# Six rows of a vector-matrix product, moved part by part between the products that make the filters' taps

## The chip, the cores and the metric

The kernel runs on one core of one Trainium2 chip. The metric is the device time of one execution in microseconds, taken as the median of several runs. Inside a core five engines run their own instruction queues in order and wait for each other by semaphores: PE (TensorE, matrix products), DVE (VectorE), ACT (ScalarE), POOL (GpSimd) and SP (SyncE, which here only issues DMAs).

## What is computed

Two transformer-like blocks are applied to one sequence of 1024 positions and 1024 channels. The part that matters here belongs to both. From the first block: the modulation row `mod = silu(c) @ mod_w + mod_b`, and a depthwise convolution of 31 taps. From the second: the Hyena filters.

```python
mod = c_act @ mod_w[i] + mod_b[i]            # (1, 1024) @ (1024, 6144)
u = causal_dwconv(u, dw_w) + dw_b            # 31 taps, 1024 channels
...
h = (hdn @ fw3 + fb3).reshape(L, HYENA_ORDER, 2, D_HYENA)   # taps of the filters: hdn (1024, 64)
h = h * jnp.exp(-t * deltas)[:, None, None, :]
...
return jnp.fft.rfft(circ, axis=0)            # their transform
```

## The kernel before

Every engine has a program of its own (`tensor_program`, `scalar_program`, ...), written out by hand, and all of them walk through the same list of steps. A planner (`Kernel.plan`) gives each result a place in a ring; `Ring.take` takes the next place and remembers what must have ended before it may be written again, and the engines turn that into semaphore waits (`hold_bank` on PE).

The stretch of the change is `OTHER` (L213 to L224): 32 filter steps `f`, 16 for each of the two orders of the filters (`o = s // 16`, `step = s % 16`), with six modulation blocks `m` of 512 output columns between them, jb 4 to 9.

- **Tap steps** (step 0 to 7). PE makes two products of taps, n = 0 and 1 (L1059, 65 rows, 512 columns, float32, each in the trace as two matmul records), each into a PSUM bank of its own. DVE multiplies each by the decay (L2294, "decay multiply"), ACT rounds it to the first half of a pair of numbers (L1554), DVE subtracts to get the second half (L2312, event `tlo`), which frees the bank. Between these DVE makes two taps of the depthwise convolution (L2256), and ACT makes two products (L1606) that POOL adds (L2715).
- **Transform steps** (step 8 to 15). PE multiplies 8 tiles of taps by one filter matrix (L776, 24 matmuls) into two banks; ACT copies one (L1560), DVE adds and subtracts (L2322 to L2326), and then makes two taps of the convolution. The matrices are split into two halves by ACT (L1367) and DVE (L1880) before that.
- **Modulation block**. Its weights come in four parts, kp 0 to 3, one raw slot of 512 KB each. `modulation` (L826) makes a 1 x 512 row: two products for each part (L837, each two records as well). Then ACT copies the row to SBUF (`modulation_row`, L1383), PE turns it (`modulation_turn`, four small transposes, L847), and DVE adds the bias (L1919, event `mod`). Only then is its bank free.

Before, a modulation block stands whole behind tap step 0, 3 or 5 of each order: all 16 records of it follow each other on PE. ACT's copy of the row comes directly behind, before the next step's work, and PE turns the row behind the first tap product of the next step. The four banks 0 to 3 are one ring, through which taps, modulation rows and transforms pass in order:

```python
bank.take(("taps", o, step, n), ("tlo", o, step, n))
bank.take(("filt", o, kt, n, 0), ("fcopy", o, kt, n))
bank.take((kind, s), *self.mod_free(kind, s))
```

Raw slots are four; SP fills slot j once part j - 4 was used (`feed`), in the same queue in which it loads the decay for two steps ahead, which waits for DVE's decay multiply.

Of the kernel before, what the change touches and what calls it, by code (L numbers as in the profile page):

```python
# [44 lines left out]
RAW = 4  # L45
HL = 3
# [177 lines left out]
OTHER = other_steps()  # L224

# [27 lines left out]
def pool_steps(s):  # L254

    return 2 if s < 24 else 0
# [65 lines left out]
class Kernel:  # L322
# [283 lines left out]
    def plan(self):  # L606
# [18 lines left out]
        bank = self.bank  # L625
# [4 lines left out]
        for kind, s in OTHER:  # L630
            if kind == "f" and SUM_STEPS.get(s):
                tmp.take(("lnsq", SUM_STEPS[s]), ("lnqadd", SUM_STEPS[s]))
            if kind != "f":
                self.mod_weights(kind, s)
                bank.take((kind, s), *self.mod_free(kind, s))
                continue
# [122 lines left out]
def tensor_program(e, k):  # L759
# [289 lines left out]
    def filter_step(s, turn):  # L1049

        o, step = s // 16, s % 16
        if step < 8:
# [3 lines left out]
            for n in range(2):  # L1056
# [4 lines left out]
                if turn and n == 0:  # L1061
                    modulation_turn(*turn)
# [34 lines left out]
    turn = None  # L1097
    for kind, s in OTHER:
        if kind == "f":
            filter_step(s, turn)  # L1100
            turn = None
        else:
            modulation(kind, s)
            turn = (kind, s)
# [247 lines left out]
def scalar_program(e, k):  # L1352
# [33 lines left out]
    def modulation_weights(kind, jb, ahead):  # L1386
        for kp in range(4):
            split_to(k.W[kind, jb, kp] + ahead)

# [237 lines left out]
    row = None  # L1627
    for kind, s in OTHER:
        if row:
            modulation_row(*row)  # L1630
            row = None
        if kind == "f":
# [4 lines left out]
        else:  # L1637
            modulation_weights(kind, s, HL)
            row = (kind, s)
# [227 lines left out]
def vector_program(e, k):  # L1867
# [60 lines left out]

    def modulation_weights(kind, jb, ahead):
        for kp in range(4):  # L1930
            split_to(k.W[kind, jb, kp] + ahead)
# [354 lines left out]
    def filter_step(s, row):  # L2286
        o, step = s // 16, s % 16
        if step < 8:
# [3 lines left out]
            for n, t in enumerate(rows):  # L2292
                w.wait_ge(*k.at("taps", o, step, n))
                e.tensor_tensor(t, t, dec, ALU.mult).then_inc(*k.to("dec", o, step, n))  # L2294
                if row and n == 0:
                    modulation_add(*row)
# [88 lines left out]
    row = None  # L2385
    for kind, s in OTHER:
        if kind == "f":
            filter_step(s, row)
            row = None
            if s in SUM_STEPS:  # L2390
                convolved_sum(SUM_ORDER.index(SUM_STEPS[s]))
        else:
            modulation_weights(kind, s, HL)
            row = (kind, s)
# [295 lines left out]
def gpsimd_program(e, k):  # L2690
# [34 lines left out]
    for kind, s in OTHER:  # L2725
        if kind == "f":
            convolve(pool_steps(s))
# [25 lines left out]
def sync_program(e, k):  # L2753
# [129 lines left out]
    for kind, s in OTHER:  # L2883
        if kind == "f":
            filter_step(s)
        else:
            feed_modulation(kind, s)
# [323 lines left out]
```

## Time and profile before

| | |
|---|---|
| median of 3 runs | 3266.72 us (3257.31 to 3267.85) |
| the profiled execution's own time | 3264.56 us |
| its span in the profile | 3262.8 us |
| PE, DVE, ACT, POOL busy | 95%, 52%, 31%, 12% of the span |
| stretch of the change in the trace | about 246 to 454 us |

### The profile page before, as it was taken

What the parts mean: (1) busy time and instruction counts of PE and PEld (TensorE: products, weight loads), DVE (VectorE), ACT (ScalarE), POOL (GpSimd) and SP (SyncE); (2) the same over time, 40 slices, a digit from 0 to 9 for tenths busy, and PEclk for the clock granted to TensorE, in tenths of its full rate; (3) what the DMA queues carried; (4) which work ended last, traced back from release to release, by engine and by line L of the source; (5) the groups of instructions that cost most, each with busy time, mean ns of one, the idle gap of its engine ahead of it and who ended that gap; (6) DMA issues with size and microseconds to landing.
All of it is one profiled execution on the core that took longest, in us unless ns stands there. A gap on an engine that the chain in (4) does not pass through costs nothing. (4 is left out here: it accounts for less than half of the span.)

```text
span 3262.8 us, 33626 instructions
## 1 busy us (share of the span) xinstructions
PE 3093.9 (95%) x13786; PEld 2490.5 (76%) x13786; DVE 1709.1 (52%) x1863; ACT 1016.5 (31%) x1222; POOL 389.5 (12%) x158
## 2 busy tenths in 40 slices
PE   7999889899999999989999999799999999999997
PEld 3784468678888887878888877687877788888886
DVE  5698885755656554674511076677556322222225
ACT  3456543332212122233221133576222311111111
POOL 0498700000000000000200144000110000000000
PEclk8998889899999999999999999999998999999998
DMA  6115423231222422122333343521431202112112
GB/s 208 59 33 161 152 94 123 81 118 60 87 94 84 136 83 87 70 84 78 130 109 103 116 153 124 138 62 51 138 110 55 75 27 65 46 42 62 33 52 110
DMA packets 97217, 301.25 MB, mean 92 GB/s; under 512 B 11205, under 2 KB 15045, under 8 KB 96871
## 3 DMA queue, kind: packets, MB, share of 16 engines
q1 hardware_dynamic: 97064, 299.09, 28.1%
q8 instruction: 110, 1.80, 0.2%
q14 instruction: 43, 0.35, 0.0%
HBM read 251.34 MB, written 47.71 MB: 92 GB/s over the span
## 5 line engine op out<-in xcount | busy, mean ns | idle before, releaser
L776 PE MATMUL ps<-mainr,wh 128*128 128x512 f32 (+1 forms) x6592 | 1791.7, 390 | 24.0 <-issue 10.8
L776 PEld LDWEIGHTS ps<-mainr,wh 128*128 128x128 f32 x6592 | 1236.1, 189 | 282.3 <-issue 28.9
L776 PE MATMUL ps<-mainr,wl 128*128 128x512 f32 (+1 forms) x3296 | 1039.6, 389 | 0.0
L776 PEld LDWEIGHTS ps<-mainr,wl 128*128 128x128 f32 x3296 | 622.3, 189 | 128.6
L1880 DVE TENSOR_TENSOR wl<-raw,wh 128x1024 fp32r<-128x1024 f32 (+2 forms) x264 | 292.6, 1111 | 458.9 <-ACT wh L1367 458.6
L1367 ACT CAST wh<-raw 128x1024 fp32r<-128x1024 f32 (+2 forms) x312 | 280.4, 903 | 738.1 <-PE ps L776 537.8
L2256 DVE SCALAR_TENSOR_TENSOR ps<-mainf,vec,ps 128x1024 f32<-128x1024 f32 (+1 forms) x174 | 181.0, 1103 | 2.5 <-ACT ps L1594 2.3
L2735 POOL TENSOR_TENSOR tmp<-tmp,mainf 128x1024 f32<-128x1024 f32 x8 | 27.5, 3442 | 1205.7 <-DMA mainf<-in_rope 1143.8
L2221 DVE TENSOR_TENSOR mainf<-mainf,ps 128x1024 f32<-128x1024 f32 x64 | 78.1, 1220 | 177.0 <-PE ps L776 177.0
L822 PE MATMUL ps<-mainr,wh 128*128 128x512 f32 x480 | 137.8, 411 | 29.7 <-issue 17.9
L1182 PE MATMUL ps<-mainr,wh 128*128 128x512 f32 x512 | 159.5, 393 | 6.2 <-POOL wl L2702 6.0
L2702 POOL TENSOR_TENSOR wl<-raw,wh 128x1024 fp32r<-128x1024 f32 x48 | 114.8, 2401 | 423.5 <-ACT wh L1367 423.5
L822 PEld LDWEIGHTS ps<-mainr,wh 128*128 128x128 f32 x480 | 94.2, 199 | 54.9 <-issue 29.6
L1489 ACT CAST mainr<-tmp 128x1024 fp32r<-128x1024 f32 x44 | 46.2, 1049 | 281.3 <-DVE tmp L2202 214.7
L2187 DVE SCALAR_TENSOR_TENSOR tmp<-ps,vec,tmp 128x1023 f32<-128x1023 f32 x44 | 56.3, 1280 | 136.6 <-ACT tmp L1472 136.5
L2202 DVE TENSOR_TENSOR tmp<-ps,tmp 128x1024 f32<-128x1024 f32 x22 | 26.9, 1224 | 183.7 <-PE ps L776 182.6
L2593 DVE TENSOR_REDUCE cols<-ps 128x1 f32<-128x1280 f32 x64 | 95.0, 1486 | 46.5 <-PE ps L1247 46.4
L1182 PEld LDWEIGHTS ps<-mainr,wh 128*128 128x128 f32 x512 | 96.4, 189 | 27.2 <-issue 6.8
L1247 PE MATMUL ps<-mainr 128*128 128x512 f32 (+1 forms) x384 | 96.9, 390 | 15.5 <-DMA mainr<-sc_k 7.9
L1472 ACT ACTIVATE tmp<-ps,vec 128x1024 f32<-128x1024 f32 x44 | 52.9, 1204 | 179.5 <-PE ps L776 179.5
L837 PE MATMUL ps<-raw,cols 128*1 128x512 f32 x160 | 84.0, 684 | 20.8 <-DMA raw<-in_mod_w 15.3
L1182 PE MATMUL ps<-mainr,wl 128*128 128x512 f32 x256 | 100.1, 391 | 0.0
(265 smaller groups left out, 2890.6 us busy)
## 6 DMA issues: line engine op xcount, KB each, us to landing
raw<-in_mod_w SPq DMA_DIRECT2D x48, 512.0 KB, 4.3
raw<-in_ada_w SPq DMA_DIRECT2D x48, 512.0 KB, 3.7
raw<-in_f_up SPq DMA_DIRECT2D x44, 512.0 KB, 4.2
raw<-in_g_up SPq DMA_DIRECT2D x44, 512.0 KB, 3.5
raw<-in_w_in SPq DMA_DIRECT2D x40, 512.0 KB, 4.1
raw<-in_pw SPq DMA_DIRECT2D x24, 512.0 KB, 3.8
sc_x<-mainf SPq DMA_DIRECT2D x24, 512.0 KB, 2.6
mainf<-sc_x SPq DMA_DIRECT2D x24, 512.0 KB, 6.7
```

Of the source, the lines that this page charges most:

```text
L776: ins = e.matmul(out, wt[:, a:b], xs[n], start=kk == 0 and t == 0, stop=kk == kt - 1 and t == 2)
L822: ins = e.matmul(out, wt[:, a:b], xs[n], start=kk == 0 and t == 0, stop=kk == kt - 1 and t == 2)
L837: ins = e.matmul(bank[0:rows, 0:512], lhs[:, kk * rows:(kk + 1) * rows], k.RAWT(j)[:, 512 * n:512 * n + 512], start=kk == 0, stop=kk == 7)
L1182: ins = e.matmul(out, wt[:, a:a + 128], x, start=first and t == 0, stop=last and t == 2)
L1247: ins = e.matmul(k.SC[i][:, a:b], k.q_at[u % 3][:, 128 * qt:128 * qt + 128], k.k_at[u % 3][t][:, a:b], start=t == 0, stop=t == 1)
L1367: e.copy(k.WH(j), k.RAWT(j)).then_inc(*k.to("whi", j))
L1880: e.tensor_tensor(k.WL(j), k.RAWT(j), k.WH(j).bitcast(F32), ALU.subtract).then_inc(*k.to("wlo_dve", j))
L2187: e.scalar_tensor_tensor(out=t[:, 1:T], in0=ps[:, 0:T - 1], scalar=k.V("fdw", 3 * f + 1), in1=t[:, 1:T], op0=ALU.mult, op1=ALU.add).then_i ...
L2221: e.tensor_tensor(y(i), y(i), k.ACC(s + "_dn", c, i), ALU.add).then_inc(*k.to("yadd", s, c, i))
L2256: e.scalar_tensor_tensor(out=out[:, a:b], in0=k.U(i)[:, tap + a:tap + b], scalar=k.V("dww", TAPS * i + tap), in1=k.CVP(i)[:, a:b], op0=ALU ...
L2593: e.tensor_reduce(k.STAT(n, i), k.SC[i], AX.X, ALU.max, negate=True).then_inc(*k.to("atmax", n, i))
L2702: e.tensor_tensor(k.WL(j), k.RAWT(j), k.WH(j).bitcast(F32), ALU.subtract).then_inc(*k.to("wlo_pool", j))
```

## The change

The list with the modulation blocks between the steps is gone; each part of a block has a place of its own behind a product of taps, from a table.

```diff
-def other_steps():
-
-    mods = iter([("m", j) for j in range(4, 10)])
-    out = []
-    for s in range(32):
-        out.append(("f", s))
-        if s % 16 in (0, 3, 5):
-            out.append(next(mods))
-    return out
+MOD_PARTS = (((0, 0), (0, 1), (1, 0), (1, 1)), ((2, 1), (3, 0), (3, 1), (4, 0)), ((5, 1), (5, 1), (6, 0), (6, 1)))
+MOD_TURNS = (2, 5, 7)
+
+
+def parts_behind(s, n):
+
+    return [(4 + 3 * (s // 16) + x, kp) for x, parts in enumerate(MOD_PARTS) for kp, at in enumerate(parts) if at == (s % 16, n)]
+
+
+def turned_in(s):
+
+    return ("m", 4 + 3 * (s // 16) + MOD_TURNS.index(s % 16)) if s % 16 in MOD_TURNS else None
```

The planner: taps use banks 0 to 2, a modulation row bank 3, transforms all four, each time from bank 0 on.

```diff
             o, step = s // 16, s % 16
+            if step % 8 == 0:
+                bank.only(*range(4 if step else 3))
             if step < 8:
                 for n in range(2):
                     bank.take(("taps", o, step, n), ("tlo", o, step, n))
+                    for jb, kp in parts_behind(s, n):
+                        if kp == 0:
+                            bank.put(3, ("m", jb), *self.mod_free("m", jb))
+                        self.weight(("m", jb, kp), d["mod_w"][4 * jb + kp], 1024, None)
```

PE, ACT (DVE has the same lines for the splits) and SP:

```diff
@@ PE
-                if turn and n == 0:
-                    modulation_turn(*turn)
+                if n == 0 and turned_in(s):
+                    modulation_turn(*turned_in(s))
+                for jb, kp in parts_behind(s, n):
+                    modulation("m", jb, (kp,))
@@ ACT
-    row = None
-    for kind, s in OTHER:
-        if row:
-            modulation_row(*row)
-            row = None
-        if kind == "f":
-            if s in SUM_STEPS:
-                convolved_square(SUM_STEPS[s])
-            filter_step(s)
-            products(pool_steps(s))
-        else:
-            modulation_weights(kind, s, HL)
-            row = (kind, s)
+    for s in STEPS:
+        if turned_in(s):
+            modulation_row(*turned_in(s))
+        if s in SUM_STEPS:
+            convolved_square(SUM_STEPS[s])
+        filter_step(s)
+        products(pool_steps(s))
+        if s % 16 in (6, 7):
+            split_to(k.W["filt", s // 16, 0, 0] + (2, 3)[s % 16 - 6])
@@ SP
+    for s in STEPS:
+        for n in range(2):
+            for jb, kp in parts_behind(s, n):
+                feed(k.W["m", jb, kp] + 1 + RAW)
+        filter_step(s)
```

The first place is PE's queue at the start of the tap steps of order 0. `ps<-mainf...,ex` is a product of taps, `ps<-raw,cols` a product of a modulation, `ps<-ident,row` the transposes of its row. Before:

```order
L1059 MATMUL ps<-mainf_0_8192_57,ex 128x512 [waits s_glu,s_fw3d,s_sin]
L1059 MATMUL ps<-mainf_0_8192_57,ex 128x512
L837 MATMUL ps<-raw_49,cols 1x512 [waits s_raw0,s_gate]
...
L837 MATMUL ps<-raw_49,cols 1x512 [waits s_raw3]
L837 MATMUL ps<-raw_49,cols 1x512
L1059 MATMUL ps<-mainf_0_8192_57,ex 128x512
L847 MATMUL ps<-ident,row 128x1 [waits s_mrow]
L847 MATMUL ps<-ident,row 128x1 x3
L1059 MATMUL ps<-mainf_0_8192_57,ex 128x512 [waits s_tlo] x2
```

And now:

```order
L1064 MATMUL ps<-mainf_0_8192_57,ex 128x512 [waits s_glu,s_fw3d,s_sin]
L842 MATMUL ps<-raw_49,cols 1x512 [waits s_raw0,s_gate]
L842 MATMUL ps<-raw_49,cols 1x512
L1064 MATMUL ps<-mainf_0_8192_57,ex 128x512
L842 MATMUL ps<-raw_49,cols 1x512 [waits s_raw1]
...
L1064 MATMUL ps<-mainf_0_8192_57,ex 128x512 [waits s_tlo]
L842 MATMUL ps<-raw_49,cols 1x512 [waits s_raw3]
L842 MATMUL ps<-raw_49,cols 1x512
L1064 MATMUL ps<-mainf_0_8192_57,ex 128x512 [waits s_tlo]
L852 MATMUL ps<-ident,row 128x1 [waits s_mrow]
```

The second tap product of step 0 now has the first part ahead of it, the fourth tap product waits for a `tlo`, and the transposes stand one step later, in step 2.

The second place is PE's queue where the tap steps of order 0 end and the first transform (`ps<-mainr...,wh`) begins. Before:

```order
L847 MATMUL ps<-ident,row 128x1 x3
L1059 MATMUL ps<-mainf_0_8192_57,ex 128x512 [waits s_tlo] x2
L1059 MATMUL ps<-mainf_0_8192_57,ex 128x512 [waits s_mod]
L776 MATMUL ps<-mainr_8192_20480_59,wh 128x512 [waits s_tlo,s_thi,s_wlo_dve,s_whi]
```

And now:

```order
L1064 MATMUL ps<-mainf_0_8192_57,ex 128x512 [waits s_tlo]
L852 MATMUL ps<-ident,row 128x1 [waits s_mrow]
L852 MATMUL ps<-ident,row 128x1 x3
L1064 MATMUL ps<-mainf_0_8192_57,ex 128x512 [waits s_tlo]
L781 MATMUL ps<-mainr_8192_20480_59,wh 128x512 [waits s_tlo,s_thi,s_wlo_dve,s_whi]
```

The waits have the same names but not the same values: the first transform took bank 3 before, last used by the first tap product of step 6; now it takes bank 0, last used by the second tap product of step 7, the last of all.

The third place is ACT's queue around the copy of the row of block 4 (`COPY row<-ps`). `CAST mainr...<-ps` rounds taps, `ACTIVATE ...<-mainf,vec` are the products that POOL adds. Before:

```order
L1554 CAST mainr_8192_20480_59<-ps 128x512 [waits s_dbadd,s_dec]
L1606 ACTIVATE mainf_0_8192_57<-mainf_24576_32768_53,vec 128x1024 [waits s_gadd] x2
L1383 COPY row<-ps 1x512 [waits s_modT,s_moduse]
L1554 CAST mainr_8192_20480_59<-ps 128x512 [waits s_dec] x2
```

And now:

```order
L1551 CAST mainr_8192_20480_59<-ps 128x512 [waits s_dec] x2
L1603 ACTIVATE st<-mainf_24576_32768_53,vec 128x1024 [waits s_gadd]
L1603 ACTIVATE mainf_0_8192_57<-mainf_24576_32768_53,vec 128x1024 [waits s_gadd]
L1384 COPY row<-ps 1x512 [waits s_modT,s_moduse]
L1551 CAST mainr_8192_20480_59<-ps 128x512 [waits s_dec] x2
```

The copy moved behind the roundings and products of step 1; those of step 2 come after it.

## Rows read from the trace of the kernel before

**Rows 1.** The page: busy time, share of the span and instructions.
```profile
PE 3093.9 (95%) x13786; PEld 2490.5 (76%) x13786; DVE 1709.1 (52%) x1863; ACT 1016.5 (31%) x1222; POOL 389.5 (12%) x158
```

**Rows 2.** Windows by stage: busy of each engine, PEclk, DMA share, GB/s.
```profile
246.00:296.00 50.00, 43.65 (x92) 10.90 (x92) 39.56 (x51) 31.07 (x38) 40.86 (x19) 0.85 0.54 173
296.00:342.00 46.00, 45.92 (x191) 37.81 (x192) 43.17 (x42) 28.34 (x32) 44.83 (x17) 0.94 0.51 162
342.00:395.00 53.00, 43.40 (x94) 11.40 (x93) 42.39 (x54) 28.39 (x36) 36.44 (x17) 0.86 0.49 173
395.00:454.00 59.00, 48.66 (x201) 39.28 (x200) 57.95 (x59) 26.54 (x31) 9.44 (x4) 0.90 0.41 134
302.00:342.00 40.00, 40.00 (x178) 33.11 (x177) 37.17 (x35) 23.86 (x27) 38.98 (x15) 1.00 0.56 179
```

**Rows 3.** Waits of PE and of DVE, 246 to 470: total, times, longest.
```profile
PE ps L879 <- DVE st L2273: 8.3, 1, 8.3
PE ps L847 <- ACT row L1383: 4.5, 3, 2.0
PE ps L837 <- DMA raw<-in_mod_w: 3.1, 1, 3.1
DVE ps L2294 <- PE ps L1059: 15.1, 9, 3.7
```

**Rows 4.** Timeline of PE, both stretches of tap steps.
```profile
248.49 7.08 PE L837 MATMUL ps<-raw,cols 128*1 128x512 f32 x16
...
258.09 0.41 PE L847 MATMUL ps<-ident,row 1*128 1x1 f32 x4 [1.46 <-ACT row L1383]
...
262.13 3.78 PE L1059 MATMUL ps<-mainf,ex 65*128 65x512 f32 x4 [0.30 <-DVE mainr L2312]
...
296.08 1.19 PE L776 MATMUL ps<-mainr,wh 128*128 128x512 f32 x2 [1.17 <-DVE mainr L2312]
...
342.29 1.88 PE L1059 MATMUL ps<-mainf,ex 65*128 65x512 f32 x4
...
395.12 1.50 PE L776 MATMUL ps<-mainr,wh 128*128 128x512 f32 x2
```

**Rows 5.** Timeline of DVE in the tap steps.
```profile
254.42 1.28 DVE L2256 SCALAR_TENSOR_TENSOR ps<-mainf,vec,ps 128x1024 f32<-128x1024 f32 x1
...
263.77 1.29 DVE L2294 TENSOR_TENSOR ps<-ps,mainf 128x512 f32<-128x512 f32 x2
...
268.55 1.29 DVE L2294 TENSOR_TENSOR ps<-ps,mainf 128x512 f32<-128x512 f32 x2
...
289.00 3.73 DVE L1880 TENSOR_TENSOR wl<-raw,wh 128x1024 fp32r<-128x1024 f32 x2 [1.61 <-ACT wh L1367]
...
299.89 1.27 DVE L2312 TENSOR_TENSOR mainr<-ps,mainr 128x512 fp32r<-128x512 f32 x2
```

**Rows 6.** Timeline of ACT, tap steps 0 and 1.
```profile
256.43 1.15 ACT L1606 ACTIVATE mainf<-mainf,vec 128x1024 f32<-128x1024 f32 x1 [1.29 <-POOL mainf L2715]
```

**Rows 7.** Timeline of DVE, order 1.
```profile
353.01 1.27 DVE L2256 SCALAR_TENSOR_TENSOR ps<-mainf,vec,ps 128x1024 f32<-128x1024 f32 x1
...
398.95 1.28 DVE L2312 TENSOR_TENSOR mainr<-ps,mainr 128x512 fp32r<-128x512 f32 x2
...
405.68 0.67 DVE L2322 TENSOR_TENSOR tmp<-tmp,ps 128x512 f32<-128x512 f32 x1
...
451.12 1.21 DVE L2273 TENSOR_TENSOR st<-st,mainf 128x1024 f32<-128x1024 f32 x1
```

**Rows 8.** Windows at the lower clock, columns as in rows 2.
```profile
261.00:270.00 9.00, 7.70 (x9) 1.63 (x9) 9.00 (x13) 5.96 (x8) 8.69 (x5) 0.50 0.21 58
295.00:301.00 6.00, 4.92 (x12) 3.89 (x13) 6.00 (x9) 4.48 (x6) 5.03 (x3) 0.50 0.32 86
391.00:400.00 9.00, 9.00 (x17) 5.16 (x16) 8.95 (x13) 5.96 (x8) 4.96 (x3) 0.50 0.00 0
```

**Rows 9.** The page's DMA issues: count, KB each, us to landing.
```profile
raw<-in_mod_w SPq DMA_DIRECT2D x48, 512.0 KB, 4.3
```

More of the change, by code:

```diff
@@ L210, in __getitem__ @@
         return self.parts[lo, hi][rows, a - lo:b - lo]
-def other_steps():
-    mods = iter([("m", j) for j in range(4, 10)])
-    out = []
-    for s in range(32):
-        out.append(("f", s))
-        if s % 16 in (0, 3, 5):
-            out.append(next(mods))
-    return out
-OTHER = other_steps()
+STEPS = range(32)
+MOD_PARTS = (((0, 0), (0, 1), (1, 0), (1, 1)), ((2, 1), (3, 0), (3, 1), (4, 0)), ((5, 1), (5, 1), (6, 0), (6, 1)))
[4 more added lines that the diff above has]
+    return ("m", 4 + 3 * (s // 16) + MOD_TURNS.index(s % 16)) if s % 16 in MOD_TURNS else None
 def vector_units(group):
@@ L629, in plan @@
         tmp.only(*range(NTMP - 1))
-        for kind, s in OTHER:
-            if kind == "f" and SUM_STEPS.get(s):
+        for s in STEPS:
+            if SUM_STEPS.get(s):
                 tmp.take(("lnsq", SUM_STEPS[s]), ("lnqadd", SUM_STEPS[s]))
[L633 to L636, printed above, removed]
             o, step = s // 16, s % 16
+            if step % 8 == 0:
+                bank.only(*range(4 if step else 3))
             if step < 8:
@@ L1047, in hidden_layer, with filter_step @@
         ins.then_inc(*k.to("hid", layer))
-    def filter_step(s, turn):
+    def filter_step(s):
         o, step = s // 16, s % 16
@@ L1094, in tensor_program @@
         tile(("pw1", n), 8, x, ready)
-    turn = None
-    for kind, s in OTHER:
-        if kind == "f":
-            filter_step(s, turn)
-            turn = None
-        else:
-            modulation(kind, s)
-            turn = (kind, s)
+    for s in STEPS:
+        filter_step(s)
     hold_aux("cols", "ln", banks=(0,))
@@ L1384, in modulation_row @@
         row_before = (kind, jb)
-    def modulation_weights(kind, jb, ahead):
-        for kp in range(4):
-            split_to(k.W[kind, jb, kp] + ahead)
     def root(s, eps, event, scale=1.0, src=m.ps[:, 3072:3080]):
@@ L1626, in scalar_program @@
         products(POOL_TAPS[i] - POOL_TAPS[i] // 2)
-    row = None
-    for kind, s in OTHER:
-        if row:
-            modulation_row(*row)
-            row = None
-        if kind == "f":
-            if s in SUM_STEPS:
-                convolved_square(SUM_STEPS[s])
-            filter_step(s)
-            products(pool_steps(s))
-        else:
-            modulation_weights(kind, s, HL)
-            row = (kind, s)
+    for s in STEPS:
+        if turned_in(s):
[6 more added lines that the diff above has]
+            split_to(k.W["filt", s // 16, 0, 0] + (2, 3)[s % 16 - 6])
     assert made == len(POOL_ORDER)
@@ L1927, in modulation_sum_add @@
                                    in1=k.V(base, 4 * jb, 4), op0=ALU.mult, op1=ALU.add).then_inc(*k.to("mod", kind, jb, r))
-    def modulation_weights(kind, jb, ahead):
-        for kp in range(4):
-            split_to(k.W[kind, jb, kp] + ahead)
     def hold_mod(kind, jb):
@@ L2284, in filter_pairs, with filter_step @@
         e.scalar_tensor_tensor(out=b, in0=b, scalar=-2.0, in1=f, op0=ALU.mult, op1=ALU.add).then_inc(*k.to("fw3d", 1))
-    def filter_step(s, row):
+    def filter_step(s):
         o, step = s // 16, s % 16
@@ L2294, in filter_step @@
                 e.tensor_tensor(t, t, dec, ALU.mult).then_inc(*k.to("dec", o, step, n))
-                if row and n == 0:
-                    modulation_add(*row)
+                if n == 0 and turned_in(s):
+                    modulation_add(*turned_in(s))
             if step == 0:
@@ L2384, in vector_program @@
             filter_pairs()
[L2385 to L2394, printed above, removed]
+    for s in STEPS:
+        filter_step(s)
+        if s % 16 in (6, 7):
+            split_to(k.W["filt", s // 16, 0, 0] + (2, 3)[s % 16 - 6])
+        if s in SUM_STEPS:
+            convolved_sum(SUM_ORDER.index(SUM_STEPS[s]))
     conv_steps(turns, 1000)
@@ L2724, in gpsimd_program @@
         convolve(POOL_TAPS[i])
-    for kind, s in OTHER:
-        if kind == "f":
-            convolve(pool_steps(s))
+    for s in STEPS:
+        convolve(pool_steps(s))
     assert added == len(POOL_ORDER)
@@ L2882, in sync_program @@
                 decay(0, step)
[L2883 to L2887, printed above, removed]
+    for s in STEPS:
+        for n in range(2):
+            for jb, kp in parts_behind(s, n):
+                feed(k.W["m", jb, kp] + 1 + RAW)
+        filter_step(s)
     feed(k.W["pw2", 0] + 1)
```

## The prediction

> **What bounds the kernel now.** First the page: PE is busy for 95% of the span [rows 1], so at most places PE sets the time, and a gain on another engine is worth something only where PE waits for it. Next, windows cut at the stages of the change [rows 2]. Between 246 and 454 us there are four stages: tap steps of order 0 (A), transforms of order 0 (B), tap steps of order 1 (C), transforms of order 1 (D). The reader is to see three things. In A and C PE has records for 43.7 of 50 and 43.4 of 53 us, at a mean clock of 0.85 and 0.86; in B it is busy all the time; in D DVE is, 57.95 of 59 us. The waits [rows 3] say what each stage hangs on: PE waits once for 8.3 us for DVE's last sum (L2273), right behind D, so the end of this stretch is DVE's end in D. DVE for its part loses 15.1 us in nine waits for tap products (L1059). The row of a modulation, copied by ACT, costs PE 4.5 us in three waits, and a late weight 3.1 us once.
>
> So the path is: A (PE and DVE by turns), B (PE), C (by turns), D (DVE). Stages B, C and D begin on PE at 296.1, 342.3 and 395.1, and A just ahead of 248.5 [rows 4], and the end is 452.3, when L2273 has run (451.12 + 1.21) [rows 7].
>
> **Prices.** A modulation block is 16 records in 7.08 us at the full clock, 0.443 a record, so a part (4 records) is 1.77 us and a tap product (2 records) 0.89 [rows 4]. At the lower clock four tap records took 3.78 us [rows 4], 0.945 each, twice as much. A transform matmul is 40.00 / 178 = 0.225 us at the full clock [rows 2]. DVE needs 268.55 - 263.77 = 4.78 us for a tap step [rows 5], with no wait inside it.
>
> **What the change takes away.** PE's work does not change: per order 16 tap products, 24 modulation products, three row turns of 0.4. Gone is the long run of 16 records that lets DVE run dry (its longest wait for taps is 3.7 us [rows 3]). Gone too is the 3.1 us wait for a weight in C: SP now requests it before it waits for a decay multiply. I price the new requests at nothing: each raw slot is asked for again when its part is used, and the next use is at least four parts, over 7 us, away, against 4.3 us to landing [rows 9].
>
> **What it adds, at the full clock.** I walk the queues of A in their new order.
>
> 1. Tap product (0,1) stands behind a part, 1.77 us later, and with the hand-over DVE's second decay multiply is 2.0 late; DVE ends step 0 not at 254.42 + 1.19 = 255.6 [rows 5] but at 257.6. In C this costs nothing, since DVE comes from its last transform later than PE.
> 2. PE now runs ahead of ACT. The row of block 4 is complete when PE ends step 1 (about 258.3), but ACT copies it only behind the products of step 1, the second of which waits for POOL as such products do now: one begins at 256.43 after a wait for POOL, [rows 6], and POOL takes 2.2 to 2.6 us an addition [rows 2], say 4.9 for two, so the next such one begins at 261.3. The copy is out at 262.9, PE turns the row, and tap product (2,1), behind it, is ready at 264.3. PE stands still for 3.8 us, DVE loses 1.6 in step 2.
> 3. In steps 3 to 5 tap product (s,1) stands behind a part or a turn and is 0.5 late each: 1.5 together. In step 6 it has three parts and two tap products ahead of it since step 5: 2.1 late.
> 4. The splits of the first two filter matrices stay ahead of DVE's last step: 3.73 us for two [rows 5]; bounds are 2.4 (two passes of 1.21 as in rows 7) and 3.73 for one of them alone beside POOL.
> 5. The first transform now needs bank 0, freed by the last `tlo` of step 7. Before it needed that of step 6, a whole DVE step earlier.
>
> DVE's last `tlo` of A: 257.6 + 7 x 4.78 - 1.2 (the last convolution tap lies behind it) + 1.6 + 1.5 + 2.1 + 3.7 = 298.8. Before it ended at 299.89 + 1.27 = 301.2 [rows 5], so DVE wins 2.4 us. But PE had started transforms at 296.1 and now starts at 298.8: **A +2.7**.
>
> B is 24 matmuls x 8 x 0.225 = 43.2 at the full clock, and was 46.2 because it began at the lower one [rows 8]. PE stands still for over 3 us twice just before its new start (for the last row, then for the last `tlo`), so it will begin at the lower clock again: **B 0**.
>
> C in the same way, counted on the old axis: step 0 on DVE ends at 353.01 + 1.19 = 354.2 as before; 354.2 + 33.5 - 1.2 + 3.7 + 4 x 0.5 + 2.1 = 394.3 for the last `tlo`, before 398.95 + 1.28 = 400.2 [rows 7]. PE starts D at 394.4, before 395.1. D: DVE must now wait for the first tile. 12 matmuls at half clock and 12 at full are 8.1 us, copy 0.5: first addition at about 403.0, before 405.68 [rows 7]; from there it runs 46.6 us without a wait. **C and D together -2.7.**
>
> So at a full clock in the tap steps the sum is 0.0.
>
> **The clock.** Before, in A the mean of 0.85 over 50 us means 15 us at half clock, 0.86 over 53 us in C about as much; without the pieces at the transforms' starts (295 to 301, 391 to 400 [rows 8]) some 24 us are left, four stretches of 6 on average, the longest over 9 (261 to 270). Its beginning follows PE's wait of 1.46 at 258.09 and steps of taps alone [rows 4, 8]. The new order puts a longer wait, about 3.5 us, ahead of each row turn. And what follows the turns of blocks 4 and 5 is the densest part: steps 3 and 5 to 6 hold two parts each, PE needs 2 x 0.89 + 2 x 1.77 = 5.3 us a step against DVE's 4.78, so there is no slack, and a stretch of 6 us at half clock makes DVE 3 us late. I take four such stretches, 2.8 us each: **+11.3**. Bounds: four of half that length give +6, four as long as the longest +19. That is the unknown that sets the range.
>
> The Trainium skill warns of more: its page "TensorE: Matmul & The Clock Gate", section "A second HAM failure mode: psum-queue depth-cycling", says that a PE that cycles through PSUM banks with small idle gaps between groups keeps falling back to the lower clock. The rows agree in part: in A PE stood still for 6 of 50 us in pieces under 2 us and spent 15 us at half clock. A ring of three banks instead of four makes more such gaps; taken whole, the rule would give the last rival below.
>
> **Sum.** 3264.56 (the profiled execution; 2.2 below the median of three) + 2.7 + 0 - 2.7 + 11.3 = 3275.9, so **3276 us**. Outside of this stretch nothing changes.
>
> **Rivals.** A measurement of this kernel can tell about 0.3% from no change, 9.8 us.
>
> - *Forecast, +6 to +19*: chance 0.57; three quarters of it lie beyond 9.8.
> - *The clock stays up*. Modulation products use all 128 rows and now stand between the tap products, and no step 1 to 6 consists of taps alone. For: block 4's 16 records, at 248.49, all ran at the full clock [rows 4]. Against: the new waits of 3.5 us. Then the sum is 0.0: 3265 us. It decides from where the four stretches cost less than 2.4 each. Chance 0.28.
> - *Other sign: DVE never runs dry*. If ACT's copies came in time and every tap product too, DVE would lose none of its 15.1 us for taps, and A would end 8 us, C 9 us earlier on DVE; PE's starts of B and D follow DVE's last `tlo`, so they gain 3.7 and about 7: 3254 us. Against: the copy is queued behind POOL's pace, whatever PE does. It decides when the turns are less than 1 us late. Chance 0.08.
> - *Half clock nearly throughout*: steps 2 to 7 have 26 us of PE work at the full clock, 52 at half, against some 34 on DVE: +18 in each of A and C, 3300 us. Against: PE waited in A and C before too, and the mean was still 0.85 [rows 2]. Chance 0.07.
> - *No effect because the work was hidden*: excluded, since PE and DVE wait for each other in A and C.
>
> Range for 8 in 10: from just under the case of the clock that stays up, 3262, to 3285, which leaves out the last rival, most of the third and the forecast's end. Chances: faster 0.08; slower 0.45 + 0.07 = 0.52; within 0.3% the rest, 0.40.
>
> **What would show it.** Row copies: PE waits for `row` three times in each order, over 2.5 us each. PE's first transform waits for a `tlo` for 3 us or more, in both orders. DVE waits for `tmp` over 2 us before its first addition in B and D. The weight's wait (3.1) is gone. No single wait of DVE for taps over 3 us at the full clock. The mean clock over the tap steps stays at 0.85 or falls. It is wrong if the windows of A and C show a clock above 0.95, or if the row copies are not late.

## The result, and the profile after

The changed kernel takes 3279.7 us (median of the runs; 3278.0 to 3283.3, one disturbed run left out), the kernel before, run beside it, 3262.8 us (3257.3 to 3267.9). The ratio is 1.0053, with a 95% interval of 1.0041 to 1.0065: slower by 0.5%, some 17 us. The prediction had 3276 us, 11.3 above the 3264.6 it started from.

The profiled execution of the changed kernel is the one of 3279.7 us; its span is 3277.9 us, 15.1 more than before. The page's first rows hardly move: PE is busy for 2.5 us more and has the same 13786 instructions as in [rows 1].

```profile
span 3277.9 us, 33623 instructions
PE 3096.4 (94%) x13786; PEld 2487.1 (76%) x13786; DVE 1710.3 (52%) x1863; ACT 1015.0 (31%) x1222; POOL 391.8 (12%) x158
```

The windows by stage answer to [rows 2] (columns as there), with one row more for all that comes behind:

```profile
244.00:305.00 61.00, 46.96 (x92) 10.01 (x92) 45.92 (x57) 34.22 (x42) 45.16 (x20) 0.82 0.43 138
305.00:351.00 46.00, 45.49 (x190) 37.51 (x191) 37.35 (x36) 24.94 (x28) 40.03 (x15) 0.94 0.48 154
351.00:414.00 63.00, 49.04 (x95) 10.54 (x94) 48.61 (x60) 31.11 (x40) 41.84 (x19) 0.80 0.44 146
414.00:471.00 57.00, 46.68 (x192) 37.52 (x192) 50.19 (x52) 22.46 (x27) 5.59 (x2) 0.92 0.41 136
471.00:3278.00 2807.00, 2689.56 (x12330) 2233.95 (x12330) 1355.07 (x1471) 797.14 (x985) 130.07 (x48) 0.97 0.27 87
```

The reader is to see that both stages of tap steps have grown, the first to 61 us, the second to 63, and that the granted clock in them fell to 0.82 and 0.80. PE has about the same number of records there as before, but is busy for longer (46.96 us for the 92 of A, 43.65 before).

The stages' starts on PE and the last sum on DVE, exactly, from two timelines (PE, then DVE), beside [rows 4] and [rows 7]:

```profile
244.84 1.20 PE L1064 MATMUL ps<-mainf,ex 65*128 65x512 f32 x2 [1.54 <-DVE mainf L2364]
...
261.98 0.40 PE L852 MATMUL ps<-ident,row 1*128 1x1 f32 x4 [2.17 <-ACT row L1384]
...
280.50 0.58 PE L852 MATMUL ps<-ident,row 1*128 1x1 f32 x4 [3.10 <-ACT row L1384]
281.01 2.08 PE L1064 MATMUL ps<-mainf,ex 65*128 65x512 f32 x2
283.01 5.39 PE L842 MATMUL ps<-raw,cols 128*1 128x512 f32 x8
...
298.17 0.58 PE L852 MATMUL ps<-ident,row 1*128 1x1 f32 x4 [2.98 <-ACT row L1384]
298.68 2.08 PE L1064 MATMUL ps<-mainf,ex 65*128 65x512 f32 x2
305.51 1.19 PE L781 MATMUL ps<-mainr,wh 128*128 128x512 f32 x2 [4.75 <-DVE mainr L2301]
...
351.50 1.02 PE L1064 MATMUL ps<-mainf,ex 65*128 65x512 f32 x2
```

```profile
303.98 1.27 DVE L2301 TENSOR_TENSOR mainr<-ps,mainr 128x512 fp32r<-128x512 f32 x2
...
469.70 1.21 DVE L2262 TENSOR_TENSOR st<-st,mainf 128x1024 f32<-128x1024 f32 x1
```

The last stage starts on PE at 414.81, behind a wait like the one at 305.51. So the stages last, A to the start of the last sum: 60.7, 46.0, 63.3 and 54.9 us, 224.9 together. Before, with A starting on PE at 246.61, they lasted 49.5, 46.2, 52.8 and 56.0 us, 204.5 together. All of the loss is in A (+11.2) and C (+10.5); B and D give 1.3 us back, which leaves 20.4 us in this pair of traces.

The waits between 246 and 490 us answer to [rows 3]: total, times, longest.

```profile
DVE ps L2283 <- PE ps L1064: 27.6, 15, 3.6
DVE tmp L2311 <- ACT tmp L1557: 16.6, 7, 6.1
PE ps L852 <- ACT row L1384: 16.5, 6, 3.1
PE ps L781 <- DVE mainr L2301: 9.5, 2, 4.8
```

PE waits for ACT's row 16.5 us where it waited 4.5; a new wait for DVE's last tap split (L2301), 4.8 us, stands ahead of the first transform of each order (in order 0 only such a wait of 1.17 us stood there before [rows 4]); DVE waits for taps 27.6 us where it waited 15.1. The wait for a weight's DMA is gone. In the timeline of PE above, the eight products of block 6 at 283.01 take 5.39 us: at the lower clock, behind a turn that had waited 3.10.

How much of the four stages ran at half clock I read from windows of 1 us (twice the share missing to 1.00, added up): 40.9 us before, 58.1 us after (the end of D, where TensorE only waits for the last sum, is not counted). Every kernel below is described by these two readings of its trace: the length of the four stages (from A's first tap product on PE to the start of the last sum, 204.5 before) and the low time in them (40.9).

Low time is not all the edit's. A begins behind the same wait of 1.54 us in each of the 14 traces of this study, yet the clock fell within some 2 us of A's start in six of them (the changed kernel and experiments 1, 5, 8, 10 and the three fillers of 7) and stayed up in eight (the kernel before and the others). In the changed kernel's trace this is 3.4 of the 58.1 us: its first part took 3.43 us, where experiment 2, with the same code there, took 1.88.

### The profile page after: what moved, and what is told of

It reads as the page before. It is cut to its first block and busy times, and to the rows that moved or that the text cites. A ratio compares the mean times of both kernels' runs of the same rounds, so it can differ in the third digit from the quotient of the medians.

```text
span 3277.9 us, 33623 instructions
## 1 busy us (share of the span) xinstructions
PE 3096.4 (94%) x13786; PEld 2487.1 (76%) x13786; DVE 1710.3 (52%) x1863; ACT 1015.0 (31%) x1222; POOL 391.8 (12%) x158
## 5 line engine op out<-in xcount | busy, mean ns | idle before, releaser
L1486 ACT CAST mainr<-tmp 128x1024 fp32r<-128x1024 f32 x44 | 46.2, 1049 | 281.6 <-DVE tmp L2191 214.7
L2700 POOL TENSOR_TENSOR mainf<-mainf,mainf 128x1024 f32<-128x1024 f32 x40 | 99.0, 2475 | 29.7 <-ACT mainf L1591 14.0
```

Of the source, the lines that this page charges most:

```text
L2700: e.tensor_tensor(k.CV(i), k.CV(i), k.PROD(added), ALU.add).then_inc(*k.to("gadd", i, tap))
```

## The experiments

**Theory.** The loss is made of two waits of TensorE: for bank 0 ahead of the first transform, and for the late row copies. Each is a short stop behind which TensorE is granted half the clock, and this makes it larger. **Rivals.** The loss comes from three banks as such; or from the parts between the taps; or the clock carries it alone, whatever waits.

Each experiment has its ratio to the kernel before, run beside it. That kernel's own median was between 3262.6 and 3265.8 us from group to group, so a difference of two medians from different groups is sure to some 3 us only; where the ratios say something else, both are given.

**1. The ring's order turned, `e1_banks`.** The ring that the transforms go through is turned (and the taps of order 1 begin one bank later), so that the first transform's bank is one which step 6 frees, not step 7. The taps still have three banks.

```
-                bank.only(*range(4 if step else 3))
+                r = (1, 2, 0) if o else (0, 1, 2)
+                bank.only(*((r[1], 3, r[2], r[0]) if step else r))
```

> The changed kernel, but the transforms take their banks in another order: first those of the second tap product of step 6 and of the modulation row, then those of step 7; order 1 begins its taps on bank 1. Theory 1 (the wait of PE's first transform for the last tlo costs, in both orders, 3 to 5 us on the path in A and 4 to 6 in D, where DVE waits for the first tile): PE's wait before its first transforms shrinks from over 4 us to under 1.5, DVE's 6 us waits before its first addition shrink to about 2, the time falls by 6 to 10 us against the changed kernel, to about 3271, 0.25% above the kernel before. Rival (late row copies and the lower clock after them carry all of it): the time stays within 2 us of the changed kernel's 3280.

Measured: 3271.2 us, ratio to before 1.0019 [1.0011, 1.0028]; 8.5 us below the changed kernel. In its trace the stages last 211.8 us, the low time is 40.9, and the first transform begins right behind the last tap product:

```profile
299.49 0.58 PE L853 MATMUL ps<-ident,row 1*128 1x1 f32 x4 [2.99 <-ACT row L1385]
300.00 2.08 PE L1065 MATMUL ps<-mainf,ex 65*128 65x512 f32 x2
301.09 1.42 PE L782 MATMUL ps<-mainr,wh 128*128 128x512 f32 x1
```

So the order of banks costs half of the loss by the medians and some two thirds, 11 us, by the ratios (1.0053 and 1.0019), and low time is 17 us less with it. The waits for rows are as they were (16.5 us in six).

**2. The row copied early, `e2_row`.** ACT copies the row ahead of the products of the step before, not behind them. Everything else is as in the changed kernel.

```
-        if turned_in(s):
-            modulation_row(*turned_in(s))
         if s in SUM_STEPS:
             convolved_square(SUM_STEPS[s])
         filter_step(s)
+        if turned_in(s + 1):
+            modulation_row(*turned_in(s + 1))
         products(pool_steps(s))
```

> The changed kernel, but ACT copies the row of a modulation directly behind the roundings of the step in which its last part stands, ahead of the two products for POOL. Theory 1: PE's six waits for the row (16.5 us in all, 3.1 the longest) shrink to at most 1 us each where DVE is not late itself, but DVE sets the pace in most steps, so the time falls by only 1 to 4 us, unless the lower clock after the turns goes with the waits, then by up to 8: 3272 to 3279. Rival (the late copy is the main cost): it falls by over 10 us, to about 3268 or below.

Measured: 3280.7 us (3273.2 to 3284.1), ratio 1.0046 [1.0033, 1.006]: no gain, against my expectation. The waits of its trace (same window and columns as above) show where it went:

```profile
PE ps L781 <- DVE mainr L2301: 20.0, 2, 10.0
PE ps L852 <- ACT row L1384: 2.0, 2, 1.0
```

TensorE comes earlier to the first transform and waits there, 10 us each time, for the same tap split. While bank 0 hangs on the last step, most of what TensorE wins ahead of it doesn't count. Whether all of it is lost stays open: the six runs lie 11 us apart, and the profiled one is the fastest of them (3273.2 us), with stages of 217.9 us against 224.9.

**3. Both, `e5_banks_row`.** The turned ring of 1 and the early copy of 2 together.

> The changed kernel with both edits of the first two runs: transforms take their banks in the other order, and ACT copies the row ahead of its products. The row copy alone moved nothing, and PE then waited up to 10.0 us for the last tlo. Theory 1 (the late copies cost only where no later wait absorbs what is won; with the transform's wait gone they count): faster than the bank order alone by 2 to 6 us, about 3267, level with the kernel before. Rival (the copies are hidden behind DVE's pace whatever follows): the same as the bank order alone, 3271.

Measured: 3264.6 us, ratio 1.0007 [0.9998, 1.0016]: the time of the kernel before. The early copy, worth nothing measurable alone, is worth 6.5 us by the medians (4 by the ratios) when the bank's wait is gone. The two edits leave the parts between the taps and the three banks in place, so these two together need not cost anything. That does not clear either by itself: experiment 5 has the three banks without the parts between the taps, and loses.

**4. Three banks alone, `e6_three_banks`.** The kernel before, with the modulations whole as they were, but in bank 3, and the taps in the other three.

```
-                bank.take((kind, s), *self.mod_free(kind, s))
+                bank.put(3, (kind, s), *self.mod_free(kind, s))
                 continue
             o, step = s // 16, s % 16
+            if step % 8 == 0:
+                bank.only(*range(4 if step else 3))
```

> The kernel before with the banks of the changed one alone: modulation blocks stay whole behind steps 0, 3 and 5, but take bank 3; taps use banks 0 to 2, transforms all four from bank 0 on. Theory 1 (a ring of three and the wait for the last tlo cost by themselves): slower than before by 10 to 18 us, about 3277, that is, the banks alone bring most of the loss, and the spreading of parts gives a few us back at best. Rival (the spreading is what costs, since second tap products and row turns come late): within 3 us of the kernel before, 3263.

Measured: 3278.3 us, ratio 1.0042 [1.0029, 1.0056]: nearly the changed kernel's time, without one part moved. The first transform waits for the split here as well, 3.5 us in each order:

```profile
PE ps L778 <- DVE mainr L2314: 7.0, 2, 3.5
PE ps L849 <- ACT row L1385: 3.5, 3, 1.4
```

The banks alone bring most of the loss; making the modulations in parts changed little on top (1.4 us by the medians, 3.6 by the ratios, within what the runs tell).

**5. Three banks in the turned order, `e8_whole_banks`.** As 4, with the order of 1.

> The kernel before with blocks whole, taps in three banks, rows in bank 3, and the transforms in the better bank order. It stands to the run with three banks alone as the changed kernel with that order stands to the changed kernel. Theory 1 (the bank order is worth the same with or without spreading, and spreading itself is worth nothing to within 3 us): 3269 to 3272, like the changed kernel with the same order. Rival (spreading is worth a gain once the wait of the transforms is gone): over 4 us slower than that kernel, above 3275.

Measured: 3274.5 us, ratio 1.0031 [1.002, 1.0041], between the two expectations. Two comparisons matter. Against 4 the turned order gives back 3.8 us, not 8.5. Against the kernel before, which has the same whole modulations but four banks, this one is 10.9 us slower, with an interval clear of no change, although no transform waits for a tap split and the row waits come to 3.1 us. So here the missing bank itself costs, and what grew in the trace is TensorE's wait for a split that frees a bank for taps (this kernel, then 1, then the kernel before):

```profile
PE ps L1062 <- DVE mainr L2315: 12.3, 8, 1.7
PE ps L1065 <- DVE mainr L2302: 2.4, 2, 1.7
PE ps L1059 <- DVE mainr L2312: 1.2, 2, 0.9
```

Against 1, which has the same banks and the parts spread, it is 3.3 us slower: a ring of three seems to suit spread parts better than whole ones. The runs of this kernel lie 10 us apart (3265.7 to 3275.8, the lowest being the profiled one), so these sizes are rough.

**6. An early request in the kernel before, `e7_early`.** Only the other thing that the change does: SP asks for the weight of order 1 ahead of its wait.

```
+            if s == 16:
+                feed(k.W["m", 7, 3] + 1)
             filter_step(s)
```

> The kernel before with one line of SP moved: the last weight of block 7 is requested before SP waits for DVE's decay multiply of step 16. Theory 1 (this part of the change is a gain that the rest of it covers): PE's wait of 3.1 us for the weight is gone, DVE's wait of 2.9 before its next decay multiply shrinks, and the time falls by 2 to 4 us against the kernel before. Rival (another wait takes its place, since PE only reaches DVE's or ACT's queue earlier): the same as before within 1 us.

Measured: 3262.2 us, ratio 0.9998 [0.9989, 1.0007]: no difference. The wait of 3.1 us for the DMA is gone from its trace, and TensorE's waits for rows are 8.9 us instead of 4.5:

```profile
DVE ps L2294 <- PE ps L1059: 14.2, 10, 3.9
PE ps L847 <- ACT row L1383: 8.9, 4, 3.0
```

Another wait takes its place. So in the kernel before the weight's wait was worth nothing; in the changed kernel it was not tried by itself.

**7. The clock: useless products ahead of each turn, `e3_fill` and `e10_fill_two`.** In the changed kernel TensorE stands still for 2 to 3 us ahead of the row turns. Here it makes three (then two) 128x512 products of constants there, into the bank that the step's second tap product will overwrite.

```
                 if n == 0 and turned_in(s):
+                    hold_bank("taps", o, step, 1)
+                    for _ in range(3):
+                        e.matmul(k.BANK("taps", o, step, 1), m.ident[:, :], m.vec[:, 0:512], start=True, stop=True)
                     modulation_turn(*turned_in(s))
```

> The changed kernel with 18 products added that nobody reads: ahead of each row turn PE makes three 128 x 128 by 128 x 512 products of constants (2.7 us at the full clock) into the bank of the step's second tap product, which overwrites them. They fill the waits for the row copies with work. Theory 1 (the low clock after each turn's wait costs 2 to 3 us each in steps 3, 5 and 6, and some at the transforms' starts): the stretches at half clock behind the turns of blocks 4, 5, 7 and 8 vanish or shrink, and although PE has 16 us more work the time falls by 4 to 10 us, to 3270 to 3276. Rival (the waits themselves cost, the clock is a by-product without price): the time stays at 3280 or rises by up to 5 us.

Measured: 3279.4 us, ratio 1.0044 [1.0032, 1.0056]. The low time fell from 58.1 to 27.3 us, and the time did not follow. The timeline of PE shows both halves of it:

```profile
279.16 4.54 PE L1069 MATMUL ps<-vec,ident 128*128 128x512 f32 x6 [1.71 <-DVE mainr L2304]
283.63 0.40 PE L852 MATMUL ps<-ident,row 1*128 1x1 f32 x4
283.96 1.12 PE L1064 MATMUL ps<-mainf,ex 65*128 65x512 f32 x2
285.02 3.59 PE L842 MATMUL ps<-raw,cols 128*1 128x512 f32 x8
```

The eight products behind the turn are at the full clock, 3.59 us instead of 5.39; but the turn comes at 283.63 instead of 280.50, since the fillers first wait 1.71 us for their bank and then last 4.54 us, longer than the rest of the wait that they fill. With two:

> The changed kernel with two fillers per turn and nothing else. With three it took 3279.4 us, as without. Theory (the first transform's wait for bank 0 and the late taps take up what the clock gives): 3276 to 3281 us. Rival (three fillers delayed the turn, two don't, and the clock then gives here what it gave with the bank order): 3266 to 3272 us.

Measured: 3274.9 us (3271.9 to 3276.4), ratio 1.0035 [1.0023, 1.0048]: 4.8 us below the changed kernel, just outside of the expectation of no gain and well short of the other. Its low time is 20.4 us, and its first transforms wait 5.9 us each for the split. That wait swallows most of what the clock gives: the same fillers gave 11.6 us where the wait is gone, in experiment 8.

**8. Fillers with the turned order, `e4_banks_fill`.** Two fillers per turn on top of 1.

> The bank order of the first run with 12 unread products of constants ahead of the six row turns, two for each (1.8 us at the full clock). Three of them without the bank order removed half of the time at half clock and gained nothing, because the turns themselves came up to 3 us later. Theory 1 (the lower clock behind the turns has a price of 2 to 3 us per stretch): with fewer fillers the turns are late by less, the stretches at half clock shrink from 41 us to below 25, and the time falls by 3 to 8 us against the bank order alone, to 3263 to 3268. Rival (the lower clock has no price here, DVE sets the pace): 3271 or above.

Measured: 3259.6 us, ratio 0.9982 [0.9973, 0.9991]: 11.6 us below 1, more than I expected, and faster than the kernel before, with twelve useless products in it. The windows by stage:

```profile
245.00:296.00 51.00, 45.89 (x103) 10.95 (x104) 39.63 (x51) 31.55 (x38) 42.85 (x19) 0.97 0.50 160
296.00:342.00 46.00, 46.00 (x195) 37.50 (x195) 45.63 (x42) 28.10 (x31) 40.81 (x16) 0.96 0.49 158
342.00:392.00 50.00, 44.54 (x106) 10.89 (x104) 43.04 (x54) 28.85 (x36) 41.75 (x18) 1.00 0.56 187
392.00:448.00 56.00, 46.38 (x195) 37.16 (x194) 55.90 (x58) 25.18 (x30) 7.10 (x3) 0.94 0.42 140
```

The mean clock of C is 1.00. Between 1 and this, low time fell by 30.7 us (40.9 to 10.2) and the stages by 11.0 us (211.8 to 200.8): 0.36 us for each us at half clock. Both traces have A's beginning at the lower clock, so it is not in the difference.

**9. All three, `e9_banks_row_fill`.** One filler per turn on top of 3.

> The changed kernel with the bank order, the early row copy and one filler product ahead of each turn. The bank order with the early copy alone took 3264.6 us; in its trace 37.5 us of the stages ran at half clock, and two fillers per turn took 30.7 us of such time and 11.6 us of the kernel's time away from the bank order alone. Theory (the clock has a price, and TensorE's short waits bring it down): one filler still takes a good part of the low time away, 3254 to 3260 us. Rival (the fillers only paid because they lay in the wait for the row copy, which is gone here, so that they now stand ahead of the turn): 3264 to 3268 us.

Measured: 3257.8 us (3255.8 to 3260.8), ratio 0.9983 [0.9974, 0.9992]. This is the fastest kernel of the study. It is 6.9 us below 3 for six products of 0.9 us; low time 37.5 to 17.1 us. The turns follow the fillers without a wait:

```profile
277.34 2.01 PE L1070 MATMUL ps<-vec,ident 128*128 128x512 f32 x2 [1.71 <-DVE mainr L2305]
279.28 0.58 PE L853 MATMUL ps<-ident,row 1*128 1x1 f32 x4
279.79 2.08 PE L1065 MATMUL ps<-mainf,ex 65*128 65x512 f32 x2
281.80 4.81 PE L843 MATMUL ps<-raw,cols 128*1 128x512 f32 x8
```

Here the clock had fallen all the same, at the filler itself (2.01 us for two records, behind a wait of 1.71 for its bank).

**10. Fillers in the kernel before, `e11_before_fill`.**

> The kernel before with two filler products ahead of each turn. 40.9 us of its four stages ran at half clock. Theory (the clock's price is there whatever stands in the banks): 3252 to 3258 us, faster than before by 5 to 11 us. Rival (the kernel before has its parts behind the turn and VectorE waits for their taps; work ahead of the turn only makes it later): 3262 to 3268 us.

Measured: 3267.4 us, ratio 1.0014 [1.0005, 1.0023]: slower by some 4 us, as the rival had it. The low time in its stages is 37.6 us, hardly less than 40.9: it fell at other places than the turns. At the very start of A it fell as it did in five other traces, and block 4 took 9.38 us instead of 7.08; and it was low at a whole modulation, block 5, as in the kernel before (9.18 us here, 8.96 there):

```profile
269.63 9.18 PE L837 MATMUL ps<-raw,cols 128*1 128x512 f32 x16 [2.79 <-DVE mainr L2315]
279.70 1.88 PE L1064 MATMUL ps<-vec,ident 128*128 128x512 f32 x4
```

So this run doesn't say that the clock has no price in the kernel before; it says that these fillers didn't buy it back there, and cost their own length.

**11. Fillers in the wait for bank 0, `e12_fill_transform`.** In the changed kernel, two products of constants in bank 3, the modulations' own, ahead of the first transform of each order.

```
+        if step == 8:
+            hold_bank("filt", o, 0, 1, 1)
+            for _ in range(2):
+                e.matmul(k.BANK("filt", o, 0, 1, 1), m.ident[:, :], m.vec[:, 0:512], start=True, stop=True)
         hold_weight(j)
```

> The changed kernel with two useless products of constants ahead of the first transform of each order, in the bank of the modulations, in the 4.75 us in which TensorE stands there waiting for the last tap split. They delay nothing that TensorE could do earlier; the question is what the low clock at the start of the transforms costs by itself. In the changed kernel 5.0 us of the first transform (305.5 to 310.5) and 4.8 us of the second (414.8 to 419.6) ran at half clock. Theory (the clock's price sits there as well): half of these 9.8 us comes back, 4.9 us, 3273 to 3277 us. Rival (the start of the transforms is bound by the evictions, or the clock doesn't rise for two products): 3278 to 3281 us.

Measured: 3277.4 us, ratio 1.0045 [1.0031, 1.0058]. This one is inconclusive: three of its six runs took 3272.2 to 3272.9 us and three 3281.9 to 3283.2, so its median is the middle of a gap. The profiled run is of the upper three, yet its stages are 8.2 us shorter than the changed kernel's: all that makes it slow lies outside of them (3064.6 us against 3053.0).

```profile
304.92 3.78 PE L1076 MATMUL ps<-vec,ident 128*128 128x512 f32 x4 [1.56 <-DVE cols L1916]
308.13 1.42 PE L781 MATMUL ps<-mainr,wh 128*128 128x512 f32 x2
309.35 0.63 PE L781 MATMUL ps<-mainr,wl 128*128 128x512 f32 x1
```

The fillers themselves run at half clock (0.945 us a record) and the transform is at the full clock from about 310 on, 2 us behind its start instead of 5. The mechanism is there; what it is worth by itself stays open. The low time of C, all but its end ahead of the second pair of fillers, is 12 us here and 25 in the changed kernel, though the code is the same there: so much can low time differ between two executions.

The kernels side by side; times are medians, stages and low time those of the one profiled run:

```
kernel                              median us   stages us   low time us
before                                3262.8      204.5        40.9
changed                               3279.7      224.9        58.1
1  turned order                       3271.2      211.8        40.9
2  early row                          3280.7      217.9        44.4
3  turned order, early row            3264.6      207.4        37.5
4  before, three banks                3278.3      217.8        54.6
5  before, three banks, turned        3274.5      211.9        51.2
6  before, early request              3262.2      203.1        37.5
7  changed, three fillers             3279.4      221.5        27.3
7  changed, two fillers               3274.9      213.8        20.4
8  turned order, two fillers          3259.6      200.8        10.2
9  turned order, early row, 1 filler  3257.8      201.8        17.1
10 before, two fillers                3267.4      213.2        37.6
11 changed, fillers at bank 0         3277.4      216.7        34.2
```

What lies outside of the stages, the same in all of these kernels, took 3052.0 to 3058.3 us in these traces, and 3064.6 in that of 11. So a single pair of traces is read for the place of a loss, and the medians for its size.

## Why the prediction was right, step by step

Sign and the main views were right: 3276 against 3279.7 us, and the forecast (slower by 6 to 19 us) holds. The predicted loss was 11.3 us, the measured one 16.9. But the sum was nearer than its terms: the two waits were foreseen, their price on the path at the full clock came to 0.0 in the sum, and the clock was priced too high. That these two errors partly cancelled is luck.

**Stage A, +2.7 predicted.** All five steps of its walk are in the trace, and steps 1, 3 and 4 are mis-sized. The row copies are late behind ACT's products, as step 2 has it, by 2.17, 3.10 and 2.98 us; it had 3.8 for the first. Step 5, the first transform's wait for bank 0, is there in both orders (4.75 us). What failed is the end of the walk: it had DVE's last tap split done at 298.8, and it was done at 305.25 (303.98 + 1.27), 307.0 counted from A's start as before. Part of this is bad luck: A began at the lower clock in this trace, and DVE's second multiply of step 0 waited 3.64 us where I had 2.0. The two splits of step 4 took 4.87 us instead of 3.73, in C too. Most of the rest is late taps: behind its first, DVE's waits for them in A come to 13.3 us where the walk has 7.2 (in C 12.8, where it has 4.1). Many of them came at half clock, which I had put into a term of its own. (The walk also adds 1.19 us where the rows of DVE say 1.28; 1.19 is the distance to the next row.)

**Stages C and D, -2.7 predicted.** D indeed became a little shorter (54.9 against 56.0 us), and DVE waits 6.1 us for ACT's copy of the first tile before its first addition, as predicted. The first addition in D starts 8.7 us behind D's start (predicted 8.6). But PE was to start D 0.7 us earlier than before, and C became 10.5 us longer instead. The term mis-sized is the same as in A, and for the most part it is bank 0. I had priced it at the full clock as a shift of the transform's start by +2.7 and -0.7 us. Experiment 1 takes it away and nothing else: A is shorter by 5.7 us (54.96 against 60.67), C by 7.3 (56.02 against 63.31), the median by 8.5 (11 by the ratios).

**Stage B, 0 predicted.** 46.2 and 46.0 us: right.

**The clock, +11.3 predicted.** It fell as predicted and at the places given (behind longer waits ahead of the turns; most in the parts that follow the turns of blocks 5 and 8, as at 283.01 above). Low time rose by 17.2 us, 3.4 of it at A's start. By the price of experiments 1 and 8, 0.36 to 0.38 us for each us of it (11.0 and 11.6 over 30.7), this is an estimated 6 us, not 11.3. In the changed kernel itself two fillers took 37.7 us of low time away for 4.8 us, 0.13 each, so 6 is the upper end of what the runs bear out. The term was too large by 5 us or more, and what bank 0 and the late rows cost by themselves, 0.0 in the sum, is then some 11 us or more. Strictly the two can't be added: without the wait for bank 0 the low time is back at 40.9 (experiment 1), so the wait's price is for a good part the clock's.

**The rule on cycling through PSUM banks** (the Trainium skill, page "TensorE: Matmul & The Clock Gate", section "A second HAM failure mode: psum-queue depth-cycling"), taken whole, gave the rival of 3300 us. The rows bear out its direction: TensorE with small gaps between groups keeps falling to the lower clock (0.82 and 0.80 in A and C). That fewer banks mean more of it was my inference, not the page's, and the rows leave it in part open: with three banks and the turned order the low time is that of four banks, 40.9 us, if the parts are spread (experiment 1), but 51.2 if the modulations are whole (experiment 5). Of these 51.2, 6.8 lie at A's start, ahead of any wait for a bank.

**What was removed.** The wait for the weight is gone. The prediction counted it among what is taken away and gave it no term; alone it is worth nothing (experiment 6). The long run of sixteen records is gone too, and DVE still waits more for taps than before (27.6 against 15.1 us).

**The rivals.** The clock that stays up: refuted by the windows. DVE never dry: refuted, 27.6 us of waits. But both describe kernels that can be made from this one: experiment 9 gets the row in time and holds the clock better, and is 22 us below the changed kernel.

**What would show it.** Held: the transform's wait of 3 us or more in both orders, DVE's wait for `tmp`, the DMA's wait gone, the clock at 0.85 or lower. Not quite: the row's waits were to be over 2.5 us each, and the first of each order is 2.17. DVE's longest wait for taps, 3.6 us, came at the lower clock, as the condition allowed.

In one sentence: the change loses because keeping a bank for the modulations leaves the taps a ring whose turn falls so that the first transform needs the bank of the very last tap step, and because the rows are copied late; each makes TensorE stop for 2 to 5 us, and behind most of these stops it goes on at half clock. Turning the ring and the early copy on top account for 15 of the 17 us together; the share of each is 8.5 and 6.5 by the medians, 11 and 4 by the ratios.

## What to carry to other kernels

When a ring of buffers loses a member, walk it to the next stage and see whose last use the first taker now waits for: with the parts spread the rotation cost 8.5 us of 17, and it is two lines. Then look at whether the smaller ring suffices at all: with spread parts it did (experiment 3), with whole modulations it cost 10 us or more in both rotations (experiments 4 and 5). When two waits lie in a row on one engine, taking the first away may show nothing until the second is gone (experiment 2 alone: nothing clear of the spread; behind experiment 1: 6.5 us), so test them together before dropping one. Where TensorE stops for some 2 to 3 us in front of dense work, a product of constants of no more than the wait's length can be cheaper than the stop, if it doesn't delay what stands behind it; too many of them (three for two), or elsewhere than the stop, give it back.

## What the runs showed that I had not expected

Useless work on TensorE made the kernel faster: twelve float32 products of 0.9 us, ahead of the row turns, took 11.6 us off (experiment 8 against 1), and six took 6.9 us off (9 against 3).

The price of the lower clock is not one half of its duration. Where TensorE and VectorE wait for each other, 30.7 us at half clock cost 11.6 us; with the wait for bank 0 in place 37.7 us cost 4.8 (experiment 7, two fillers).

The same wait does not always bring the clock down. TensorE stands for 1.54 us ahead of A in every trace; behind it the clock fell in six of them and not in the other eight.

Executions of one kernel on one chip differ by up to 11 us, in two groups for one of the kernels (3272 and 3283 us in experiment 11). A part of it lies where the change does nothing: behind the last sum the changed kernel's profiled run takes 2807.0 us and the kernel before 2810.5 (from 470.9 and 452.3 to the spans' ends), though nothing there differs, so the whole span's difference of 15.1 us hides a loss of 18.6 us ahead of that point (20.4 in the stages, less 1.8 by which A began earlier).
